# Expert stages: gathers and first weights earlier; ffn stages: two up chunks before the norm's root, first tap on ScalarE

## The chip, the cores and the metric

The kernel runs on one core of a Trainium2 chip. The metric is the device time of one execution in microseconds, taken as the median of several runs. TensorE multiplies matrices, VectorE, ScalarE and GpSimd work on SBUF (the first two on PSUM too), and SyncE (SP) issues nearly all transfers of weights.

## The reference

A small model in two blocks, one after the other, on 256 tokens of width 1024 (`x` is kept transposed, 8 tiles of 128 features). What is computed, cut to what matters:

```
first block:   x += g1 * MLA(modulate(norm(x)))             # with 256 context tokens
               x += g2 * MoE_0(modulate(norm(x)))           # 32 experts, top 2 in one of 4 groups
               x += g1 * short_conv(modulate(norm(x)))
               x += g2 * MoE_1(modulate(norm(x)))
               x = norm(x)
second block:  x += mamba2(norm(x));             x += ffn_0(norm(x))
               x += dilated_attention(norm(x));  x += ffn_1(norm(x))
               y = norm(x)

expert(t) = (silu(t @ w_gate) * (t @ w_up)) @ w_down
ffn(h)    = (silu(gate) * val) @ w_down,   gate, val = causal_conv3(h @ w_up)   # 2 x 2816 columns
norm(x)   = x * rsqrt(mean(x*x) + 1e-6) * gain
```

All data are float32. The tolerance asks for more than one pass of TensorE's rounded format, so the dense products use split values.

## The kernel before

**Engines and stages.** Each engine has one program, a list of stages: mla, expert stage 0, conv, expert stage 1, ssm, ffn 0, dilated, ffn 1. The order of the work on each engine is the order in which a stage's method writes it, and each engine executes its program in that order. Engines meet through counting semaphores; `at(name)` is the count at which a named step is done. `k.meet` at a stage's head waits for the end of the stage before on all four engines.

**Split products.** A weight chunk of 2 MiB is fetched into a ring of six 2 MiB slots by SP. ScalarE rounds it (`round_scalar`, L297, or in four pieces, `round_piece_scalar`, L312) into the next slot, VectorE subtracts (`rest_vector`, L303, in pieces L320), and a product is three passes: high weights by high values, high by low, low by high (`product3`, L584). `first_linear3_tensor` (L618, L619, L624) does the same for a stage's first chunk, k tile by k tile, as the values come. Values are split in the same way: ScalarE rounds (L680), VectorE subtracts (L668).

**Norms.** Squares of the residual tiles are made by ScalarE as the tiles come (in most stages GpSimd adds them, L487), TensorE adds over the features (L495, L497), ScalarE takes the root (L652), VectorE the reciprocal (L657), and then VectorE scales the eight tiles (L661, L699).

**Expert stage.** The router's logits and 80 small VectorE operations give places and shares. The rows of four experts (a team) are gathered by products with a 0/1 matrix (`gather`, L1307) and copied from PSUM by VectorE (`turned_x`, L1668). The four banks in which all experts' results are summed are opened by a product with zeros (`open_tensor`, L1344) between the ranks and the first gather. Then for every expert: gate and up (L1328), transposes, down (L1337), sum (L1352). Expert weights take half slots in order; SP waits for the half to be free (L347). Each stage has a further part behind a branch, for experts with more than 64 rows; the flag is zero here. The next stage's first chunk is fetched by that stage, behind the branch, and its pieces 0 and 1 are rounded by ScalarE around the root.

**Ffn.** Eleven up chunks of two output rows m each (128 gate and 128 value features per row), then six down chunks. TensorE leaves gate and value of a row in one PSUM bank. ScalarE copies it (L2744, L2749) to `PB`; VectorE makes three taps (L2783 the first, L2786 the other two, for gate and value); ScalarE takes silu (L2726); GpSimd multiplies (`h`, L2808); ScalarE rounds (L2728); GpSimd subtracts (L2810). In ScalarE's program row m's turn is: round a chunk (m even), silu and high part of row m-2, copy of row m. The down product begins by waiting for the bank of every row.

Of the kernel before, what the change touches and what calls it, by code (L numbers as in the profile page):

```python
# [16 lines left out]
P = 128  # L17
# [3 lines left out]
HALF = SLOT // 2  # L21

# [479 lines left out]
class Kernel:  # L502
# [102 lines left out]
    def first_linear3_tensor(self, e, w, chunk, outs, weights, values, n_k, tiles, pieces=False):  # L605
# [6 lines left out]
        for i in range(n_k):  # L612
# [51 lines left out]
    def norm_parts_vector(self, e, w, tag, value, gain, high, low, chunk=None):  # L664
# [5 lines left out]
        for k in range(KD):  # L670
            self.norm_value_vector(e, w, tag, k, value, gain)
            if chunk and k % 2 and k > 1:
                chunk.rest_piece_vector(e, w, k // 2)
# [13 lines left out]
    def modulated_parts_vector(self, e, w, tag, layer, T, high, low, chunk=None):  # L687
# [9 lines left out]
        for k in range(KD):  # L697
# [3 lines left out]
            if chunk and k % 2 and k > 1:  # L701
                chunk.rest_piece_vector(e, w, k // 2)
# [514 lines left out]
class Moe:  # L1217
    def __init__(self, k, layer, T, cap, before):
# [12 lines left out]
        self.slots, self.zero = ar.take(P), ar.take(P)  # L1231
        self.zeros_by = k.mats[:, 0:4, :].rearrange("p m n -> p (m n)")
# [31 lines left out]
    def sync(self, e, w):  # L1264
# [8 lines left out]
        self.k.ring.close_halves()  # L1273
        self.more_sync(e, w)
# [81 lines left out]
    def tensor(self, e, w):  # L1356
# [38 lines left out]
        w.wait_ge(*pool.at(key, "zero"))  # L1395
        for b in range(KD // 2):
            _, emptied = banks.next(dve, key, "acc", b)
            banks.hold(key, "acc", b)
            w.wait_ge(*emptied)
        self.open_tensor(e)  # L1400
# [50 lines left out]
        for part in range(KD // 2):  # L1451
            gather(0, part)
        for x in range(EXPERTS):
# [21 lines left out]
    def scalar(self, e, w):  # L1475
# [52 lines left out]
        self.then.first_chunk().round_piece_scalar(e, w, 0)  # L1528
        k.root_scalar(e, w, ("moe", layer), SEQ, eps=NORM_EPS * NORM_EPS if layer else NORM_EPS)
        self.then.first_chunk().round_piece_scalar(e, w, 1)  # L1530
        act.mark("end", key)

    def vector(self, e, w):
# [157 lines left out]
        for x in range(EXPERTS):  # L1691
# [7 lines left out]
            if x % TEAM == TEAM - 1 and x // TEAM + 2 < EXPERTS // TEAM:  # L1699
                places_of(x // TEAM + 2)  # L1700
        w.wait_ge(*pe.at(key, "sum", EXPERTS - 1))
# [5 lines left out]
        self.then.first_chunk().rest_piece_vector(e, w, 0)  # L1707
# [1671 lines left out]
```

## Time and profile before

| | |
|---|---|
| median of 3 runs | 2243.75 us (2243.53 to 2244.0) |
| profiled execution | 2242.49 us, its span 2240.7 us |
| TensorE busy | 2109.5 us, 94% of the span |
| VectorE, ScalarE, GpSimd busy | 1003.7, 718.4, 244.7 us |
| read from memory | 613.69 MB, 274 GB/s over the span |
| mean granted TensorE clock | 0.975 of full |

The profile is of one execution. Times in rows are microseconds from the span's start. "L584" is a line of the kernel. In a timeline a row is: start, duration, engine, line, operation, output<-inputs, shape, count, and in brackets how long the engine had been idle and what released it. A row with a count above 1 merges instructions that follow each other.

### The profile page before, as it was taken

To read this page: it belongs to the slowest core of one execution; us is meant where nothing else is said; L and a number is where in the kernel's file an instruction comes from. 1 tells how busy PE (TensorE), PEld (TensorE's weight loads), DVE (VectorE), ACT (ScalarE), POOL (GpSimd) and SP (SyncE) were. 2 spreads that over 40 slices of the span, in tenths; PEclk is the share of its full clock that TensorE was granted. 3 is DMA by queue.
4 is the path that set the end of the run, shared out by engine and by line. 5 is a ranking of instruction groups with operands and counts; after the bars stand their busy time and mean duration, and the time that the engine had idled before them with its cause. 6 is when DMAs were issued, how large, how long until landed. Compare 5 with 4: busy or idle time off the path is not lost. (4 is left out here: it accounts for less than half of the span.)

```text
span 2240.7 us, 31183 instructions
## 1 busy us (share of the span) xinstructions
PE 2109.5 (94%) x13462; PEld 1481.8 (66%) x13462; DVE 1003.7 (45%) x1653; ACT 718.4 (32%) x1079; POOL 244.7 (11%) x220
## 2 busy tenths in 40 slices
PE   5999999999999898999999988997899989998998
PEld 3845744444443696444444437975899989998997
DVE  3434411111111564111111107865479846777983
ACT  3234211111111442111111118855545534444552
POOL 0000000000000000000000000046125400002540
PEclk9999899999999999999999999999999999999999
DMA  9777599999999557999999985432345454434542
GB/s 326 252 273 275 227 410 421 421 421 421 421 421 421 192 204 304 417 421 421 422 420 421 421 352 191 151 113 76 113 151 189 174 196 122 113 113 151 188 171 94
DMA packets 216208, 616.86 MB, mean 275 GB/s; under 512 B 20224, under 2 KB 107392, under 8 KB 166656
## 3 DMA queue, kind: packets, MB, share of 16 engines
q1 hardware_dynamic: 208960, 612.01, 71.0%
q10 hardware_dynamic: 7104, 2.76, 0.5%
q8 instruction: 110, 1.80, 0.3%
q14 instruction: 34, 0.28, 0.0%
HBM read 613.69 MB, written 1.05 MB: 274 GB/s over the span
## 5 line engine op out<-in xcount | busy, mean ns | idle before, releaser
L1328 PE MATMUL bank<-ring,arena 128*64 128x512 f32 x2048 | 454.4, 593 | 12.4 <-DMA ring<-in_moe_w_up 12.3
L584 PE MATMUL bank<-normed_rounded,ring_rounded 128*128 128x256 f32 x3424 | 415.5, 283 | 5.0 <-ACT normed_rounded L680 3.4
L584 PEld LDWEIGHTS bank<-normed_rounded,ring_rounded 128*128 128x128 f32 x3424 | 411.2, 189 | 6.9 <-issue 4.3
L1328 PEld LDWEIGHTS bank<-ring,arena 128*64 128x64 f32 x2048 | 149.4, 137 | 305.8 <-issue 304.9
L1674 DVE TENSOR_TENSOR arena<-arena,bank 64x512 f32<-64x512 f32 x64 | 43.6, 681 | 659.3 <-ACT arena L1498 659.3
L303 DVE TENSOR_TENSOR ring_rounded<-ring,ring_rounded 128x4096 fp32r<-128x4096 f32 (+2 forms) x66 | 286.6, 4345 | 115.2 <-ACT ring_rounded L297 115.0
L584 PE MATMUL bank<-arena_rounded,ring_rounded 128*128 128x256 f32 x2336 | 290.9, 284 | 6.8 <-ACT arena_rounded L1927 2.6
L584 PEld LDWEIGHTS bank<-arena_rounded,ring_rounded 128*128 128x128 f32 x2336 | 283.3, 190 | 9.2 <-ACT arena_rounded L1927 3.4
L297 ACT ACTIVATE ring_rounded<-ring 128x4096 fp32r<-128x4096 f32 (+2 forms) x66 | 227.7, 3450 | 39.4 <-DMA ring<-in_ffn_w_down 32.8
L1337 PE MATMUL bank<-ring,arena 128*64 128x512 f32 x1024 | 233.8, 598 | 3.8 <-ACT arena L1505 3.8
L1498 ACT ACTIVATE arena<-bank 64x512 f32<-64x512 f32 x64 | 38.1, 596 | 451.0 <-PE bank L1328 451.0
L1337 PEld LDWEIGHTS bank<-ring,arena 128*64 128x64 f32 x1024 | 67.8, 136 | 122.4 <-issue 109.6
L572 PEld LDWEIGHTS bank<-mats,arena 128*128 128x128 f32 (+2 forms) x662 | 85.0, 167 | 78.8 <-issue 66.5
L1352 PE MATMUL bank<-arena 64*128 64x256 f32 x1024 | 127.8, 388 | 1.4 <-ACT arena L1512 1.4
L1512 ACT ACTIVATE arena<-bank 128x512 f32<-128x512 f32 x64 | 38.3, 599 | 275.2 <-PE bank L1337 275.2
L572 PE MATMUL bank<-mats,arena 128*128 128x128 f32 (+2 forms) x662 | 102.9, 278 | 8.5 <-POOL arena L2414 5.4
L1352 PEld LDWEIGHTS bank<-arena 64*128 64x128 f32 x1024 | 93.2, 186 | 23.7 <-issue 11.6
L2786 DVE SCALAR_TENSOR_TENSOR arena<-arena,cols 128x256 f32<-128x256 f32 x176 | 94.4, 537 | 6.3
L2810 POOL TENSOR_TENSOR arena_rounded<-arena,arena_rounded 128x256 fp32r<-128x256 f32 x44 | 93.5, 2125 | 23.3 <-ACT arena_rounded L2728 23.3
L1307 PE MATMUL bank<-arena_rounded 128*128 128x256 f32 x512 | 78.4, 298 | 0.0
L1307 PEld LDWEIGHTS bank<-arena_rounded 128*128 128x128 f32 x512 | 65.7, 190 | 5.0 <-issue 1.2
L1505 ACT ACTIVATE arena<-bank 128x256 f32<-128x256 f32 x64 | 24.7, 386 | 132.5 <-PE bank L572 132.5
(274 smaller groups left out, 2101.4 us busy)
## 6 DMA issues: line engine op xcount, KB each, us to landing
ring<-in_moe_w_gate SPq DMA_DIRECT2D x128, 1024.0 KB, 16.6
ring<-in_moe_w_up SPq DMA_DIRECT2D x128, 1024.0 KB, 18.7
ring<-in_moe_w_down SPq DMA_DIRECT2D x128, 1024.0 KB, 18.4
ring<-in_w_mod SPq DMA_DIRECT2D x24, 2048.0 KB, 11.8
ring<-in_ffn_w_up SPq DMA_DIRECT2D x44, 1024.0 KB, 6.9
ring<-in_ssm_w_in SPq DMA_DIRECT2D x12, 2048.0 KB, 8.3
ring<-in_ffn_w_down SPq DMA_DIRECT2D x10, 2048.0 KB, 8.0
ring<-in_conv_w_in SPq DMA_DIRECT2D x6, 2048.0 KB, 9.1
```

Of the source, the lines that this page charges most:

```text
L297: e.activation(ring.rounded[(self.number + 1) % RING][:, 0:n].bitcast(F32R), ring.slots[self.number % RING][:, 0:n], ACT.Copy).then_inc(*s ...
L303: e.tensor_tensor(ring.rounded[slot][:, 0:n].bitcast(F32R), ring.slots[slot][:, 0:n], ring.rounded[(self.number + 1) % RING][:, 0:n], ALU. ...
L572: return e.transpose(out, in_, self.mats[0:rows, 0, 0:rows])
L584: end = e.matmul(out, lhs.bitcast(F32R), rhs.bitcast(F32R), start=start and n == 0 and k == 0, stop=stop and n == 2 and k == n_k - 1)
L1307: end = e.matmul(out, f[:, t, feats].bitcast(F32R), mine[:, t, hot].bitcast(F32R), start=t == 0 and f is self.f_high, stop=t == self.NT - ...
L1328: ends[i] = e.matmul(bank[rows, :], xt[:, n * KD // 2 + j, :], weights[:, j, :], start=n == 0 and j == 0, stop=n == 1 and j == KD // 2 - 1)
L1337: end = e.matmul(bank[n * cap:(n + 1) * cap, :], self.ht[x][:, k, :], weights[:, i, n * 512:(n + 1) * 512], start=k == 0, stop=k == KF - 1)
L1352: end = e.matmul(self.acc(kk), self.y[x][rows, i * P:(i + 1) * P], self.back[x][rows, :], start=False, stop=last and kk % 2 == 1)
L1512: e.activation(self.y[x % 2], banks.of(key, "y", x)[:, :], ACT.Copy).then_inc(*act.up(key, "y", x))
L1674: e.tensor_tensor(h, h, banks.of(key, "h", x)[0:cap, :], ALU.mult).then_inc(*dve.up(key, "h", x))
L2786: e.scalar_tensor_tensor(buf, self.PB[:, s, j, q:q + T], w3[:, q:q + 1], buf, ALU.mult, ALU.add).then_inc(*dve.up())
L2810: e.tensor_tensor(self.H_low[:, m, :].bitcast(F32R), self.H[:, m, :], self.H_high[:, m, :], ALU.subtract).then_inc(*pool.up(key, "h low", m))
```

## The change

- Expert stages: the zero product that opens the sum banks uses a rounded zero tile, in one pass, and stands behind the first team's four gathers. VectorE copies the four gathered parts first, and then does weights, shares and tables. The ring is advanced to a whole turn, and the next stage's first chunk is fetched ahead of the branch; ScalarE rounds its pieces 0 and 1 behind the last expert's result, and VectorE subtracts piece 0 before and piece 1 after the residual update. The loops of the branch's part are merged into one.
- Ffn stages: the stage before (`prior`) also makes `raw` = residual times gain, without the root, split in high and low. Up chunks 0 and 1 are products with `raw`; chunk 0 starts without `meet`, and closes the stage before (`close_tensor`) after its second k tile. Chunk 1 is rounded in the stage before, in pieces. Rows 0 to 3 leave PSUM on VectorE, multiplied by the reciprocal root (`normed`). Chunks 2 and on use the normed values as before; chunk 2 is rounded in turn 0 and no chunk in turn 2.
- Ffn stages: the first tap of each row, for gate and value, is a scaled copy on ScalarE.

```diff
@@ first_linear3_tensor, after the products of k tile i
+            if between and i < n_k - 1:
+                between(i)
@@ Moe.sync, Moe.open_tensor
         self.k.ring.close_halves()
+        while self.k.ring.number % RING:
+            self.k.ring.skip()
+        self.then.first_chunk().fetch(e, w)
         self.more_sync(e, w)
...
+        zero = self.zero_rounded.bitcast(F32R)
         for b in range(KD // 2):
-            e.matmul(self.k.banks.of(self.key, "acc", b)[:, :], self.zero, self.zeros_by, start=True, stop=False)
+            e.matmul(self.k.banks.of(self.key, "acc", b)[:, :], zero, across(zero, BANK // P), start=True, stop=False)
@@ Moe.tensor
-        w.wait_ge(*pool.at(key, "zero"))
-        ...
-        self.open_tensor(e)
...
         for part in range(KD // 2):
             gather(0, part)
+        w.wait_ge(*pool.at(key, "zero"))
+        ...
+        self.open_tensor(e)
@@ Moe.scalar
             result(x)
+        for q in (0, 1):
+            self.then.first_chunk().round_piece_scalar(e, w, q)
...
         self.more_scalar(e)
-        self.then.first_chunk().round_piece_scalar(e, w, 0)
         k.root_scalar(e, w, ("moe", layer), SEQ, eps=NORM_EPS * NORM_EPS if layer else NORM_EPS)
-        self.then.first_chunk().round_piece_scalar(e, w, 1)
@@ Moe.vector
-        for part, between in enumerate((weights, shared, tables, lambda: self.last_steps.close_vector(e, w))):
+        for part in range(KD // 2):
             turned_x(0, part)
-            between()
+        weights()
+        shared()
+        tables()
+        self.last_steps.close_vector(e, w)
@@ Ffn, new; called by ssm and dilated behind plain_vector and square_scalar of tile m
+    def raw_vector(self, e, w, m):
+        w.wait_ge(*k.dve.now())
+        e.tensor_scalar(self.raw[:, m, :], k.X[:, m, 0:SEQ], k.col("ffn_norm")[:, self.layer, m:m + 1], None, ALU.mult
+                        ).then_inc(*k.dve.up(self.key, "raw value", m))
+    def raw_scalar(self, e, w, m):
+        w.wait_ge(*k.dve.at(self.key, "raw value", m))
+        e.activation(self.raw_parts[0](m).bitcast(F32R), self.raw[:, m, :], ACT.Copy).then_inc(*k.act.up(self.key, "raw high", m))
+    def raw_low_vector(self, e, w, m):
+        w.wait_ge(*k.act.at(self.key, "raw high", m))
+        e.tensor_tensor(self.raw_parts[1](m).bitcast(F32R), self.raw[:, m, :], self.raw_parts[0](m), ALU.subtract
+                        ).then_inc(*k.dve.up(self.key, "raw low", m))
@@ Ffn.tensor
-        k.meet(w, self.before)
...
-        k.first_linear3_tensor(e, w, first, outs, (high, low), self.x_parts, KD, k.norm_tiles(key))
+        k.first_linear3_tensor(e, w, first, outs, (high, low), self.raw_parts, KD, self.raw_ready,
+                               between=lambda i: self.prior.close_tensor(e, w) if i == 1 else None)
         for n, chunk in enumerate(self.w_up[1:], 1):
+            values, tiles = (self.raw_parts, None) if n == 1 else (self.x_parts, k.norm_tiles(key) if n == 2 else None)
@@ Ffn.scalar, turn m
-            if m % 2 == 0:
+            if m == 0:
+                self.w_up[2].round_scalar(e, w)
+            elif m % 2 == 0 and m > 2:
                 (self.w_up + self.w_down)[m // 2 + 1].round_scalar(e, w)
...
+            w.wait_ge(*(act if m >= 4 else dve).at(key, "up", m))
+            for j in range(2):
+                e.activation(self.acc[:, s, j, :], self.PB[:, s, j, 0:T], ACT.Copy,
+                             scale=taps[:, self.layer, j * KFF + m, 0:1]).then_inc(*act.up(key, "tap", m, j))
@@ Ffn.vector, turn m
+            w.wait_ge(*act.at(key, "tap", m))
             for j in range(2):
                 buf, w3 = self.acc[:, s, j, :], taps[:, self.layer, j * KFF + m, :]
-                e.tensor_scalar(buf, self.PB[:, s, j, 0:T], w3[:, 0:1], None, ALU.mult).then_inc(*dve.up())
...
+            if m < 2:
+                normed(m + 2)
@@ Ssm.vector, last part (Dilated.vector alike, with the low parts of tiles 0 to 3 and 4 to 7 together)
+            for m in (2 * n - 2, 2 * n - 1):
+                if m >= 0:
+                    self.then.raw_low_vector(e, w, m)
             for m in (2 * n, 2 * n + 1):
                 k.plain_vector(e, w, "ssm out", m)
-        k.root_vector(e, w, "ssm out", T)
+                self.then.raw_vector(e, w, m)
+        self.then.raw_low_vector(e, w, 6)
+        self.then.raw_low_vector(e, w, 7)
+        for q in range(4):
+            if q == 2:
+                k.root_vector(e, w, "ssm out", T)
+            self.then.w_up[1].rest_piece_vector(e, w, q)
```

## Rows read from the trace of the kernel before

**Rows 1.** The page, busy time of the engines.
```profile
PE 2109.5 (94%) x13462; PEld 1481.8 (66%) x13462; DVE 1003.7 (45%) x1653; ACT 718.4 (32%) x1079; POOL 244.7 (11%) x220
```
**Rows 2.** Timelines, TensorE at the start of both expert stages.
```profile
264.79 6.65 PE L1344 MATMUL bank<-mats,arena 128*128 128x512 f32 x8 [1.90 <-DVE arena_rounded L1578]
270.87 4.47 PE L1307 MATMUL bank<-arena_rounded 128*128 128x256 f32 x32
275.27 7.09 PE L1328 MATMUL bank<-ring,arena 128*64 128x512 f32 x32
...
870.33 5.96 PE L1344 MATMUL bank<-mats,arena 128*128 128x512 f32 x8 [1.90 <-DVE arena_rounded L1578]
...
880.13 7.09 PE L1328 MATMUL bank<-ring,arena 128*64 128x512 f32 x32
```
**Rows 3.** Stretches: length, busy of PE, PEld, DVE, ACT, POOL, clock, DMA share, GB/s.
```profile
260.60:270.80 10.20, 8.30 (x17) 4.67 (x18) 3.56 (x10) 0.00 (x0) 0.00 (x0) 0.50 0.98 410
```
**Rows 4.** Waits of TensorE: us in total, times, longest.
```profile
PE bank L1328 <- DMA ring<-in_moe_w_up: 12.3, 18, 1.3
```
**Rows 5.** Timelines, ScalarE at the end of both expert stages.
```profile
742.42 3.16 ACT L432 ACTIVATE arena<-residual 128x256 f32<-128x256 f32 x8 [1.10 <-DVE residual L1713]
...
746.37 1.28 ACT L312 ACT_TABLE_LOAD   x1 [0.79 <-issue]
747.66 1.06 ACT L312 ACTIVATE ring_rounded<-ring 128x1024 fp32r<-128x1024 f32 x1
...
750.03 0.38 ACT L652 ACTIVATE rstd<-bank 128x256 f32<-128x256 f32 x1
...
1354.22 1.06 ACT L312 ACTIVATE ring_rounded<-ring 128x1024 fp32r<-128x1024 f32 x1 [1.38 <-DMA ring<-in_ssm_w_in]
...
1356.59 0.38 ACT L652 ACTIVATE rstd<-bank 128x256 f32<-128x256 f32 x1
```
**Rows 6.** First ffn's start, second ffn's last row: timeline and one stretch.
```profile
1644.09 0.55 PE L618 MATMUL bank<-normed_rounded,ring_rounded 128*128 128x256 f32 x1 [3.40 <-ACT normed_rounded L680]
...
1644.10:1649.60 5.50, 5.50 (x26) 5.50 (x27) 4.77 (x14) 5.50 (x8) 0.82 (x1) 0.50 0.46 150
...
1658.28 0.39 ACT L2744 ACTIVATE arena<-bank 128x256 f32<-128x256 f32 x1 [0.56 <-PE bank L624]
...
2051.25 0.39 ACT L2744 ACTIVATE arena<-bank 128x256 f32<-128x256 f32 x1 [0.56 <-PE bank L624]
```
**Rows 7.** Up loop of ffn 0: ScalarE's timeline; stretch of L584 alone (PE, PEld).
```profile
1704.47 3.62 ACT L297 ACTIVATE ring_rounded<-ring 128x4096 fp32r<-128x4096 f32 x1
1707.99 0.40 ACT L2726 ACTIVATE arena<-arena 128x256 f32<-128x256 f32 x1
1709.48 0.42 ACT L2728 ACTIVATE arena_rounded<-arena 128x256 fp32r<-128x256 f32 x1 [1.09 <-POOL arena L2808]
1709.81 0.58 ACT L2749 ACTIVATE arena<-bank 128x512 f32<-128x512 f32 x1
1710.28 0.41 ACT L2726 ACTIVATE arena<-arena 128x256 f32<-128x256 f32 x1
1715.11 0.42 ACT L2728 ACTIVATE arena_rounded<-arena 128x256 fp32r<-128x256 f32 x1 [4.42 <-POOL arena L2808]
...
1715.91 3.62 ACT L297 ACTIVATE ring_rounded<-ring 128x4096 fp32r<-128x4096 f32 x1
...
1738.02:1749.41 11.39, 11.39 (x98) 11.39 (x97) 1.00 0.58 186
```
**Rows 8.** Up loop of ffn 0, timelines: VectorE's L303 and GpSimd's products.
```profile
1662.21 4.42 DVE L303 TENSOR_TENSOR ring_rounded<-ring,ring_rounded 128x4096 fp32r<-128x4096 f32 x1
1663.99 3.25 POOL L2808 TENSOR_TENSOR arena<-arena 128x256 f32<-128x256 f32 x1 [19.07 <-ACT arena L2726]
...
1708.46 0.98 POOL L2808 TENSOR_TENSOR arena<-arena 128x256 f32<-128x256 f32 x1 [3.44 <-ACT arena L2726]
...
1708.76 4.97 DVE L303 TENSOR_TENSOR ring_rounded<-ring,ring_rounded 128x4096 fp32r<-128x4096 f32 x1
```
**Rows 9.** Ssm's input rows, ScalarE's timeline: copy, first tap, silu of another row.
```profile
1397.68 0.37 ACT L2321 ACTIVATE arena<-bank 128x256 f32<-128x256 f32 x1
1398.08 0.51 ACT L2324 ACTIVATE arena<-arena,cols 128x256 f32<-128x256 f32 x1
1398.49 0.49 ACT L2287 ACTIVATE arena<-arena,cols 128x256 f32<-128x256 f32 x1
```
**Rows 10.** Timeline, TensorE at the start of ffn 0's down product.
```profile
1772.94 13.25 PE L584 MATMUL bank<-arena_rounded,ring_rounded 128*128 128x256 f32 x110 [0.78 <-ACT arena L2749]
```

More of the change, by code:

```diff
@@ L21 @@
 HALF = SLOT // 2
+RAW = 8192
 D = 1024
@@ L603, in linear3_tensor, with first_linear3_tensor @@
         pe.mark("free", chunk.number)
-    def first_linear3_tensor(self, e, w, chunk, outs, weights, values, n_k, tiles, pieces=False):
+    def first_linear3_tensor(self, e, w, chunk, outs, weights, values, n_k, tiles, pieces=False, between=None):
         pe, (high, low) = self.pe, weights
@@ L1452, in tensor @@
             gather(0, part)
+        w.wait_ge(*pool.at(key, "zero"))
+        for b in range(KD // 2):
+            _, emptied = banks.next(dve, key, "acc", b)
+            banks.hold(key, "acc", b)
+            w.wait_ge(*emptied)
+        self.open_tensor(e)
         for x in range(EXPERTS):
@@ new lines, in more_tensor @@
+            with e.Fori(0, (self.n_blocks - 1) * EXPERTS, 1) as it:
+                e.wait_ge(*self.more_count("vector", it, 2))
+                awake()
+                for tile in range(KD):
+                    self.gather_tensor(e, x_turned[:, tile * self.cap:(tile + 1) * self.cap], tile, slice(0, self.cap),
+                                       self.mine[0])
+                self.back_tensor(e, turned, 0).then_inc(matmul, 1)
+                e.wait_ge(*self.more_count("vector", it, 4))
+                awake()
+                e.wait_ge(*self.more_count("landed", it, 48))
+                awake()
+                for half in range(2):
+                    tiles = slice(half * KD // 2, (half + 1) * KD // 2)
+                    end = self.gate_up_tensor(e, rows, self.rows_of(0), half, gate[:, tiles, :], up[:, tiles, :])[1]
+                end.then_inc(matmul, 1)
+                e.wait_ge(*self.more_count("vector", it, 5))
+                awake()
+                self.turn_h_tensor(e, turned, 0).then_inc(matmul, 1)
+                e.wait_ge(*self.more_count("scalar", it, 2))
+                awake()
+                self.down_tensor(e, x_turned, 0, range(KF), down).then_inc(matmul, 1)
+                e.wait_ge(*self.more_count("scalar", it, 3))
+                awake()
+                self.open_tensor(e)
+                self.sum_tensor(e, 0, True).then_inc(matmul, 1)
+                e.wait_ge(*self.more_count("vector", it, 6))
+                awake()
@@ L1892, in sync @@
     def sync(self, e, w):
-        for chunk in self.w_in + self.w_out:
+        for chunk in self.w_in[1:] + self.w_out:
             chunk.fetch(e, w)
@@ L2059, in sync @@
     def sync(self, e, w):
-        for chunk in self.w_xbc + self.w_z + self.w_out:
+        for chunk in self.w_xbc[1:] + self.w_z + self.w_out:
             chunk.fetch(e, w)
@@ L2397, in scalar @@
             self.squares.square_scalar(e, w, m, k.X[:, m, 0:T], dve.at("ssm out", m))
+            self.then.raw_scalar(e, w, m)
+            self.then.w_up[1].round_piece_scalar(e, w, m - 6)
         k.root_scalar(e, w, "ssm out", T)
+        for q in (2, 3):
+            self.then.w_up[1].round_piece_scalar(e, w, q)
         act.mark("end", "ssm")
@@ L3193, in vector @@
             k.plain_vector(e, w, "att y", m)
+            self.then.raw_vector(e, w, m)
+        for m in range(4):
+            self.then.raw_low_vector(e, w, m)
         self.then.prepare_vector(e, w)
@@ L3196, in vector @@
             k.plain_vector(e, w, "att y", m)
-        k.root_vector(e, w, "dilated out", T)
+            self.then.raw_vector(e, w, m)
+        for m in range(4, KD):
+            self.then.raw_low_vector(e, w, m)
+        for q in range(4):
+            if q == 2:
+                k.root_vector(e, w, "dilated out", T)
+            self.then.w_up[1].rest_piece_vector(e, w, q)
         dve.mark("end", "dilated")
```

121 lines of the change are left out of this document (60 added, 61 removed).

## The prediction

> **What bounds the kernel now.** I read the page first, then windows and timelines around each place that the diff touches. TensorE is busy for 94% of the span [rows 1], so time can only come from the few stretches in which it stands still, works without need or runs at its lower clock, and time is lost wherever another engine's loop becomes longer than TensorE's. Three kinds of place matter.
>
> *Start of an expert stage.* TensorE opens the four sum banks with eight f32 passes (L1344), then gathers the first team, then starts the first expert: 264.79, 270.87 and 275.27 us in the first stage, 870.33 and 880.13 in the second [rows 2]. The opening falls into a stretch in which half the clock is granted (0.50, the 1.2 GHz level) behind idle moments of TensorE, and the DMA engines, busy at 0.98 there, fill the ring [rows 3]. From the first expert on both TensorE and the queues work without a pause, and near the end TensorE begins to wait for weights, 12.3 us in 18 waits over both stages [rows 4]. Both chains hang on the first expert's start: its first half frees the ring's first slot.
>
> *Change of stage.* Behind the experts the root waits in ScalarE's queue: table load, a piece of the next chunk, another table load, root at 750.03; in the second stage the piece waits another 1.38 us for its data and the root is at 1356.59 [rows 5]. At the ffn's start TensorE waits 3.40 us and then works for 5.5 us at half clock; its first chunk's last result is fetched at 1658.28, in the second ffn at 2051.25 [rows 6].
>
> *The ffn's up loop.* One chunk (two output rows m) takes TensorE 11.39 us, without idle time. ScalarE's round of the same work goes from 1704.47 to 1715.91, 11.44 us, and is full: rounding, silu, wait for GpSimd's product, high part, copy [rows 7]. VectorE is full as well. So there are three loops of one length, and what is added to any of them shows.
>
> **The change, part by part.**
>
> 1. *Gathers ahead of the opening, opening in fp32r.* The 32 gathers can start when the low parts are there, 0.5 us behind the point where L1344 starts now. With the clock's rise about where it is (5 us into the busy stretch, between the two stages' cases), some 24 gathers go at 0.21 us (26 matmuls in 5.5 us, [rows 6]) and 8 at 0.14 (4.47 us for 32, [rows 2]), 6.2 us; the opening is then four single passes of 512 columns at full clock, twice the 256 columns of 0.116 us (98 in 11.39 us, [rows 7]), 0.9 us. The first expert starts 0.5 + 6.2 + 0.9 = 7.6 us after the old start of L1344 against 10.5 and 9.8 now: about -2.6 us, twice, -5. If the clock stays down for all of it the sum is 0.5 + 6.8 + 1.8 = 9.1, a gain of 1 each; if it never falls it is 4.6 each. VectorE's small routing work, now behind the four copies, is 4.7 us and hidden by the first expert's 7.09 us of matmuls [rows 2]. GpSimd's rounding of the zero tile is hidden by the routing. Since both chains start at the first expert, the gain reaches the stage's end.
>
> 2. *First chunk fetched ahead of the branch, two pieces rounded before the squares.* SP issues it into slot 0 behind the last weights, it lands before the last expert's end, where the queues now stand empty. On ScalarE the pieces are 2 x 1.06 us before the squares, which wait 1.10 us for VectorE today: squares 1.0 us later. Behind the branch one table load (1.28) and one piece (1.06) go: root 2.34 - 1.0 = 1.3 us earlier; in the second stage 1.38 more, 2.7. Sum -4 [rows 5]. The Trainium skill (ScalarE: Activation LUTs, Table sets: the hidden batching unit) says that copy is in every table set, by which the load at 746.37, ahead of a copy, would not be the copy's; if it vanished with it, 1.28 us more would be gained in each stage. I do not count that. The queues' order changes nothing else on SP: the later chunks of the next stage are issued earlier too, with nobody waiting for them.
>
> 3. *Up chunks without the root.* TensorE goes on with chunk 0 and closes the squares after its second k tile. Gone are the 3.40 us of waiting, about 2.5 us of half clock (5.5 us at half speed) and some of the closing's own waits. Against it: each pair of output rows in the stage before puts two more products and two subtractions on VectorE and two copies on ScalarE, 0.35 to 0.42 us each, in a chain VectorE - ScalarE - rounding - VectorE that the ssm's output loop repeats. I add up 3 us until w_up[0]'s low part is there, so TensorE waits 0.7 us, then 1.5 us for the last square. Chunk 0 ends at 1653.5 instead of 1658.3: -4.8. Behind the attention only the second half of the rows is in that chain: 2044.3 instead of 2051.2, -6.9. Chunk 1 needs its low part 8 us later than VectorE has it. Sum -11.7.
>
> 4. *Up rows leave by VectorE (first four), first tap on ScalarE.* VectorE sheds its L2783 and has room again. ScalarE gets two scaled copies per row. The nearest rows are the ssm's: a tap starts 0.40 behind its own PSUM copy and the next one 0.41 later [rows 9]; with the ffn's longer copy (0.58 plus wait) copy and taps take 0.61 + 0.82 = 1.43 us where the copy took 0.47: +1.92 us per chunk. Worse is what VectorE's room does. Today VectorE comes to its rounding difference L303 at 1708.76, 0.67 us after the rounding copy's end (1704.47 + 3.62), just behind GpSimd's start on the product for which ScalarE waits, and that wait is 1.09 us [rows 7, 8]. With four L2783 less per chunk VectorE is through its taps before the copy ends; L303 then starts with the copy's end, 0.35 us ahead of the product. The case is in the trace, at the loop's start, when VectorE was not yet behind: L303 at 1662.21 for 4.42 us, the product at 1663.99 took 3.25 us and ended 0.6 us after it [rows 8]. ScalarE's chunk then is: rounding 3.53, silu and product 5.15 (until 3.65 + 4.42 + 0.61 from the chunk's start), high 0.33, copy and taps 1.43, silu and an unblocked product 1.4 (0.47, and 0.8 to 1.0), high 0.33, copy and taps 1.43: 13.6 us, against TensorE's 11.39. The same addition over today's rows gives their 11.44.
>
> TensorE asks for the low part of a chunk two thirds into its first row. By my dates w_up[3]'s comes just in time; w_up[4] to w_up[10], seven chunks, come 2.2 us later each: 15.4 us per ffn. Then the down product cannot start before ScalarE has copied row 21, which now stands behind a blocked product, two taps and a rounding piece: about 6.0 us of idle TensorE instead of 0.78 [rows 10], +5.2, and an idle time longer than the 3.40 us before the half-clock stretch of [rows 6] should bring half clock again, +2 (0 to 3.4). Later down chunks have slack. Sum 22.6 per ffn, +45.
>
> **Sum:** -5 - 4 - 11.7 + 45.2 = +24.5 us. The profiled execution took 2242.49 us (span 2240.70 and 1.8 around it), the median is 2243.75; I add to the median: **2268 us**.
>
> **Rivals.**
> - *R1, everything hidden (the other side).* If ScalarE's chunk stays under 11.39 us, no part of item 4 shows and 20.7 us are gained: 2223 us. It needs GpSimd's product to begin before L303; then the wait is 1 us instead of 4.7, ScalarE's chunk 10.0. For it: today the order is that way round in nearly every chunk. Against it: that order hangs on the 0.67 us that VectorE is late, and item 4 takes over 1.5 us per chunk from VectorE. The Trainium skill (SBUF — State Buffer, Who interferes with whom) says that the engine which issues first holds the shared port for its whole instruction; the trace agrees, with 3.25 us against 0.98, and so by that rule too the order decides. Items 3 and 4 cancel at a chunk of 12.2 to 12.3 us or so; below that the kernel is faster.
> - *R2, the loop is longer, but less.* A chunk of 12.5 to 12.9 us (a product let in now and then, shorter taps), and TensorE's slack at the loop's start larger: +5 to +10, 2251.
> - *R3, the expert stages give nothing.* The clock rises later because the gathers are the first steady work, and the queues, not TensorE, carry the stage: +9 on the forecast, 2277. For it: TensorE's 12.3 us of waiting for weights. Against it: their chain starts at the same event.
> - *R4, worse:* half clock in every 2.2 us stall, or a late w_up[3]: 2288.
>
> **Chances:** forecast 0.60 (own range 2256 to 2280), R1 0.17, R2 0.12, R3 0.06, R4 0.05. A measurement of this kernel can tell about 0.2%, 4.5 us, from no change. Range 2247 to 2284, which leaves out R1 and half of R4. Faster 0.19 (R1 and a little of R2), same 0.04, slower 0.77.
>
> **What would show it.** Item 1: L1328 of the first expert 2 to 3 us closer to L1390 in both stages. Item 2: no L312 between the branch and the root, one table load there. Item 3: no idle TensorE before the first L618 of an ffn, clock 1.0 there. Item 4: in the up loop L303 and ScalarE's L297 every 13.6 us, GpSimd's L2808 at over 4 us once per chunk, seven waits of TensorE for L303 of about 2.2 us in each ffn, and one of about 6 us for the last copy. The forecast is wrong if L2808 stays near 1 us or L297 stays at 11.4 us.

## The result and the profile after

The changed kernel takes **2265.66 us** (median, 2260.51 to 2268.83), the kernel before 2243.64 in the same rounds: ratio 1.0099, 95% interval 1.0078 to 1.0119, 22 us slower. The forecast was 2268, range 2247 to 2284. The profiled execution took 2265.92 us (span 2263.9). TensorE's busy time is as before; what grew is what it waits for:

```profile
PE 2108.9 (93%) x13454; PEld 1484.6 (66%) x13454; DVE 981.2 (43%) x1615; ACT 754.6 (33%) x1175; POOL 242.3 (11%) x222
```

The waits of TensorE over the span (us in total, times, longest) name the places; against them the kernel before had 0.4 us in one wait for the difference of a rounded chunk, L303, which is L304 now:

```profile
PE bank L585 <- DVE ring_rounded L304: 25.6, 16, 1.8
PE bank L1333 <- DMA ring<-in_moe_w_up: 11.6, 17, 1.7
PE bank L585 <- ACT arena L2797: 11.1, 2, 5.5
PE bank L619 <- ACT normed_rounded L714: 4.2, 1, 4.2
```

Read as milestones of TensorE (starts in both timelines, us), the two profiled executions differ by:

| | before | after | difference |
|---|---|---|---|
| first expert, stage 0 | 275.27 | 271.90 | -3.4 |
| conv's first product | 753.88 | 748.16 | -5.7 |
| first expert, stage 1 | 880.13 | 876.04 | -4.1 |
| ssm's first product | 1360.35 | 1353.62 | -6.7 |
| ffn 0: chunk 0 done | 1658.08 | 1645.91 | -12.2 |
| ffn 0: down product | 1772.94 | 1780.43 | +7.5 |
| attention's first product | 1844.65 | 1854.43 | +9.8 |
| ffn 1: chunk 0 done | 2051.05 | 2052.97 | +1.9 |
| ffn 1: down product | 2165.90 | 2187.24 | +21.3 |
| last product | 2229.64 | 2252.96 | +23.3 |

**Expert stages.** TensorE's timeline at both starts (answers to [rows 2]): gathers, opening in four passes (L1350), first expert (L1333).

```profile
264.46 6.58 PE L1312 MATMUL bank<-arena_rounded 128*128 128x256 f32 x32 [2.40 <-DVE arena_rounded L1584]
270.88 1.09 PE L1350 MATMUL bank<-arena_rounded 128*128 128x512 f32 x4
271.90 7.09 PE L1333 MATMUL bank<-ring,arena 128*64 128x512 f32 x32
...
868.59 6.59 PE L1312 MATMUL bank<-arena_rounded 128*128 128x256 f32 x32 [2.41 <-DVE arena_rounded L1584]
875.01 1.10 PE L1350 MATMUL bank<-arena_rounded 128*128 128x512 f32 x4
876.04 7.09 PE L1333 MATMUL bank<-ring,arena 128*64 128x512 f32 x32
```

From the first gather to the first expert it is 7.44 and 7.45 us; the forecast was 7.1. ScalarE at both ends (answers to [rows 5]): one table load (L655) in place of two, and the second stage's root (L655) now waits for the squares' sum.

```profile
736.33 1.99 ACT L313 ACTIVATE ring_rounded<-ring 128x1024 fp32r<-128x1024 f32 x2
...
743.01 1.28 ACT L655 ACT_TABLE_LOAD   x1 [0.73 <-issue]
744.31 0.38 ACT L655 ACTIVATE rstd<-bank 128x256 f32<-128x256 f32 x1
...
1347.17 1.28 ACT L655 ACT_TABLE_LOAD   x1
1349.86 0.38 ACT L655 ACTIVATE rstd<-bank 128x256 f32<-128x256 f32 x1 [1.41 <-PE bank L451]
```

**Up loop of ffn 0.** One chunk in ScalarE's timeline, from rounding to rounding (answer to [rows 7]):

```profile
1676.25 3.61 ACT L298 ACTIVATE ring_rounded<-ring 128x4096 fp32r<-128x4096 f32 x1
1679.76 0.40 ACT L2778 ACTIVATE arena<-arena 128x256 f32<-128x256 f32 x1
1684.94 0.42 ACT L2780 ACTIVATE arena_rounded<-arena 128x256 fp32r<-128x256 f32 x1 [4.78 <-POOL arena L2881]
1685.27 0.58 ACT L2797 ACTIVATE arena<-bank 128x512 f32<-128x512 f32 x1
1685.88 0.91 ACT L2801 ACTIVATE arena<-arena,cols 128x256 f32<-128x256 f32 x2
1686.70 0.40 ACT L2778 ACTIVATE arena<-arena 128x256 f32<-128x256 f32 x1
1687.95 0.42 ACT L2780 ACTIVATE arena_rounded<-arena 128x256 fp32r<-128x256 f32 x1 [0.85 <-POOL arena L2881]
1688.28 0.58 ACT L2797 ACTIVATE arena<-bank 128x512 f32<-128x512 f32 x1
1688.89 0.91 ACT L2801 ACTIVATE arena<-arena,cols 128x256 f32<-128x256 f32 x2
1689.70 3.61 ACT L298 ACTIVATE ring_rounded<-ring 128x4096 fp32r<-128x4096 f32 x1
```

VectorE's difference and GpSimd's two products of that chunk, from their timelines (answers to [rows 8]):

```profile
1679.89 4.43 DVE L304 TENSOR_TENSOR ring_rounded<-ring,ring_rounded 128x4096 fp32r<-128x4096 f32 x1 [1.47 <-ACT ring_rounded L298]
...
1680.24 4.67 POOL L2881 TENSOR_TENSOR arena<-arena 128x256 f32<-128x256 f32 x1 [4.37 <-ACT arena L2778]
...
1687.18 0.74 POOL L2881 TENSOR_TENSOR arena<-arena 128x256 f32<-128x256 f32 x1 [1.01 <-ACT arena L2778]
```

The chunk is 13.45 us. The difference starts as soon as the rounding copy ends, 0.35 us ahead of the product, and the product takes 4.67 us instead of 0.74. TensorE's timeline shows what that leaves of its 11.39 us loop, and the down product's start (answer to [rows 10]):

```profile
1657.27 13.45 PE L585 MATMUL bank<-normed_rounded,ring_rounded 128*128 128x256 f32 x112
1670.92 11.65 PE L585 MATMUL bank<-normed_rounded,ring_rounded 128*128 128x256 f32 x96 [0.20 <-DVE ring_rounded L304]
1684.37 11.65 PE L585 MATMUL bank<-normed_rounded,ring_rounded 128*128 128x256 f32 x96 [1.80 <-DVE ring_rounded L304]
...
1780.43 9.77 PE L585 MATMUL bank<-arena_rounded,ring_rounded 128*128 128x256 f32 x61 [5.54 <-ACT arena L2797]
```

### The profile page after: what moved, and what is told of

It reads as the page before. It is cut to its first block and busy times, and to the rows that moved or that the text cites. A ratio compares the mean times of both kernels' runs of the same rounds, so it can differ in the third digit from the quotient of the medians.

```text
span 2263.9 us, 31234 instructions
## 1 busy us (share of the span) xinstructions
PE 2108.9 (93%) x13454; PEld 1484.6 (66%) x13454; DVE 981.2 (43%) x1615; ACT 754.6 (33%) x1175; POOL 242.3 (11%) x222
## 5 line engine op out<-in xcount | busy, mean ns | idle before, releaser
L1333 PE MATMUL bank<-ring,arena 128*64 128x512 f32 x2048 | 454.2, 593 | 11.8 <-DMA ring<-in_moe_w_up 11.6
L585 PE MATMUL bank<-normed_rounded,ring_rounded 128*128 128x256 f32 x3232 | 397.1, 284 | 30.0 <-DVE ring_rounded L304 25.2
L585 PEld LDWEIGHTS bank<-normed_rounded,ring_rounded 128*128 128x128 f32 x3232 | 389.6, 189 | 35.2 <-DVE ring_rounded L304 28.4
L1333 PEld LDWEIGHTS bank<-ring,arena 128*64 128x64 f32 x2048 | 149.2, 137 | 305.4 <-issue 304.0
L585 PE MATMUL bank<-arena_rounded,ring_rounded 128*128 128x256 f32 x2528 | 318.0, 286 | 16.4 <-ACT arena L2797 11.1
L304 DVE TENSOR_TENSOR ring_rounded<-ring,ring_rounded 128x4096 fp32r<-128x4096 f32 (+1 forms) x64 | 269.2, 4206 | 135.9 <-ACT ring_rounded L298 135.9
L585 PEld LDWEIGHTS bank<-arena_rounded,ring_rounded 128*128 128x128 f32 x2528 | 310.5, 193 | 18.8 <-ACT arena L2797 11.4
L298 ACT ACTIVATE ring_rounded<-ring 128x4096 fp32r<-128x4096 f32 (+1 forms) x64 | 220.4, 3444 | 44.5 <-DMA ring<-in_ffn_w_down 36.6
L2857 DVE SCALAR_TENSOR_TENSOR arena<-arena,cols 128x256 f32<-128x256 f32 x176 | 102.0, 580 | 54.5 <-ACT arena L2801 48.9
L2881 POOL TENSOR_TENSOR arena<-arena 128x256 f32<-128x256 f32 x44 | 99.5, 2260 | 133.7 <-ACT arena L2778 133.7
L1312 PEld LDWEIGHTS bank<-arena_rounded 128*128 128x128 f32 x512 | 70.4, 204 | 8.8 <-DVE arena_rounded L1584 5.1
```

Source lines behind the costliest of these rows:

```text
L298: e.activation(ring.rounded[(self.number + 1) % RING][:, 0:n].bitcast(F32R), ring.slots[self.number % RING][:, 0:n], ACT.Copy).then_inc(*s ...
L304: e.tensor_tensor(ring.rounded[slot][:, 0:n].bitcast(F32R), ring.slots[slot][:, 0:n], ring.rounded[(self.number + 1) % RING][:, 0:n], ALU. ...
L585: end = e.matmul(out, lhs.bitcast(F32R), rhs.bitcast(F32R), start=start and n == 0 and k == 0, stop=stop and n == 2 and k == n_k - 1)
L1312: end = e.matmul(out, f[:, t, feats].bitcast(F32R), mine[:, t, hot].bitcast(F32R), start=t == 0 and f is self.f_high, stop=t == self.NT - ...
L1333: ends[i] = e.matmul(bank[rows, :], xt[:, n * KD // 2 + j, :], weights[:, j, :], start=n == 0 and j == 0, stop=n == 1 and j == KD // 2 - 1)
L2857: e.scalar_tensor_tensor(buf, self.PB[:, s, j, q:q + T], w3[:, q:q + 1], buf, ALU.mult, ALU.add).then_inc(*dve.up())
```

## The experiments

Twelve runs of eleven kernels (experts_again is experts_only once more). "At like clock" is worked out: over all 162 timed executions, compared within each kernel, 0.001 of mean granted clock goes with 1.34 us, and each mean is moved by that to a clock of 0.976. There the kernel before (63 executions) is at 2241.9 and the changed one at 2264.2. This measure has a flaw: where a change itself lets the clock stay up or fall, it takes that part of the effect away.

"Behind the ssm" is a second measure, from the profiled execution alone: from the end of the ssm's last product of weights to the start of the very last product, the stretch that holds both ffn stages and the attention. The kernel before takes 590.6 us for it, the changed kernel 621.2. Four other executions with the same code there agree with 590.6 within 0.3 us; a fifth, open_f32, took 593.6. What lies ahead of the stretch differs more: the ssm's last product ends at 1625.2 to 1634.1 us in the eight profiled executions that have both of the expert stages' parts, with the opening in the rounded format.

| kernel | median us | ratio to before, 95% | at like clock | behind the ssm |
|---|---|---|---|---|
| tap_vector | 2232.67 | 0.9959 (0.9945 to 0.9973) | 2232.7 | 590.3 |
| tap_only | 2278.88 | 1.0168 (1.0151 to 1.0185) | 2275.1 | 631.2 |
| late_rest | 2257.48 | 1.0072 (1.0055 to 1.0089) | 2257.0 | 612.8 |
| gated_rest | 2244.37 | 1.0006 (0.9996 to 1.0016) | 2245.4 | 601.9 |
| experts_only | 2231.38 | 0.9947 (0.9934 to 0.9960) | 2232.8 | 590.4 |
| gather_only | 2242.77 | 0.9997 (0.9988 to 1.0005) | 2238.3 | 590.4 |
| fetch_only | 2239.88 | 0.9984 (0.9975 to 0.9993) | 2239.3 | 590.3 |
| raw_only | 2240.97 | 0.9988 (0.9976 to 0.9999) | 2240.9 | 588.3 |
| tap_four | 2229.67 | 0.9939 (0.9924 to 0.9955) | 2232.9 | 587.9 |
| pieces_rest | 2230.07 | 0.9945 (0.9932 to 0.9957) | 2231.4 | 584.9 |
| experts_again | 2231.92 | 0.9949 (0.9936 to 0.9962) | 2232.2 | 590.3 |
| open_f32 | 2240.05 | 0.9986 (0.9975 to 0.9996) | 2239.2 | 593.6 |

**tap_vector: the change without its fourth part.**

```diff
@@ Ffn.scalar, Ffn.vector, turn m, against the changed kernel
-                e.activation(self.acc[:, s, j, :], self.PB[:, s, j, 0:T], ACT.Copy, scale=taps[...])   # ScalarE
+                e.tensor_scalar(buf, self.PB[:, s, j, 0:T], w3[:, 0:1], None, ALU.mult)                # VectorE
```

The lines are shortened; VectorE's own wait for the product of row m-4, which the kernel before has, comes back with the tap.

> The changed kernel with the first tap of all rows back on VectorE; everything else of the change stays. Theory (the order of VectorE's rounding difference and GpSimd's product makes the up loop long): ScalarE's chunk falls from 13.46 us back to about 11.4 us, no wait of TensorE for the difference, the wait before the down product back to about 0.8 us; 2266 - 2 x (7 x 2.07 + 4.8 + 2.3) = about 2223 us. Rival (the four rows that leave PSUM by VectorE and the two chunks from the raw values carry a good part of the loss): 2235 to 2255 us.

2232.67 us: 33 us under the changed kernel, 10 us over the 2223 that the theory gave and 2 under the rival's range. The 13.45 us loop and the 5.5 us wait are gone. What was not foreseen is one wait, before the fourth chunk (w_up[3]) of each ffn. TensorE's timeline:

```profile
1675.85 24.37 PE L585 MATMUL bank<-normed_rounded,ring_rounded 128*128 128x256 f32 x180 [2.87 <-DVE ring_rounded L304]
```

The stretch behind that wait (length, busy of PE, PEld, DVE, ACT, POOL, clock, DMA share, GB/s):

```profile
1675.85:1679.20 3.35, 3.35 (x15) 3.35 (x16) 3.21 (x7) 2.78 (x3) 1.27 (x2) 0.50 0.90 284
```

TensorE waits 2.87 us and then works at half clock (the 1.2 GHz level), until 1682.0; in the second ffn the wait is 2.62 us. In the changed kernel it was 0.20 us. From the end of chunk 0 to the down product ffn 0 takes 120.7 us here and 114.9 in the kernel before, so the 5 us gained at chunk 0 are gone there.

**tap_only: the fourth part on the kernel before.** The same edit the other way round, nothing else.

> The kernel before with nothing changed but the first tap, for all rows on ScalarE. Theory: the loop is 13.5 us per chunk here too, stalls of about 2.1 us in 7 to 9 chunks of each ffn and about 5.5 us before each down product: 2244 + 2 x (7 to 9 x 2.07 + 4.8 + 2.3) = 2287 to 2296 us. Rival (the loss comes from the tap together with the raw chunks): within 10 us of 2244.

+37 us, 8 to 17 under what was expected. The mechanism is there unchanged (GpSimd's timeline, with its product at L2811):

```profile
1699.54 4.68 POOL L2811 TENSOR_TENSOR arena<-arena 128x256 f32<-128x256 f32 x1 [4.38 <-ACT arena L2726]
```

But TensorE enters the loop later and so waits less for the same loop of ScalarE. Its waits from 1600 to 1800 us:

```profile
PE bank L584 <- DVE ring_rounded L303: 9.7, 7, 1.8
PE bank L584 <- ACT arena L2750: 4.0, 1, 4.0
```

What counts behind a loop that ScalarE carries is when ScalarE enters it. It begins to round w_up[3] 34.1 us after the ssm's last product here and 31.0 us after it in the changed kernel, and the down product starts 151.8 and 148.6 us after it: of the 5 us that the raw chunks gain at chunk 0, about 3 are kept.

**late_rest: VectorE makes the difference behind the taps.**

```diff
@@ Ffn.vector, turn m, against the changed kernel
-            elif m % 2 == 0 and m > 2:
-                (self.w_up + self.w_down)[m // 2 + 1].rest_vector(e, w)
...
             dve.mark(key, "taps", m)
+            if m % 2 == 0 and m > 2:
+                (self.w_up + self.w_down)[m // 2 + 1].rest_vector(e, w)
```

> The changed kernel with one line moved: in the up loop VectorE makes the rounding difference of the chunk behind the two taps of row m, not before them. No engine gets more or less work. Theory (order): the difference starts some 4.9 us after the rounding copy's end, when the product of the turn is long done; the product takes 0.74 us in both turns of a chunk, ScalarE's chunk would be 9.5 us by itself and is held at TensorE's 11.39 us; the low part comes about 4.9 us later, TensorE has 0 to 2 us left for it. About 2223 us, up to 2240 us if the low part comes late. Rival (work): the two scaled copies per row add 1.92 us to a full ScalarE, 11.44 + 1.92 = 13.36 us per chunk, whatever VectorE's order: 2266 us.

2257.48: between the two, and above the 2240 allowed. Order against work is decided in the trace: all 44 products are short, and ScalarE waits for TensorE now, not for GpSimd. But a new loop has closed: TensorE's row, ScalarE's copy, taps, difference, TensorE's next chunk, 12.84 us long. The product's own rows (durations: min, median, max in ns):

```profile
L2881 POOL TENSOR_TENSOR arena<-arena x44: 735/745/975, 1653.1 to 2185.4; 128x256 f32<-128x256 f32 x44
```

TensorE's timeline:

```profile
1686.54 11.66 PE L585 MATMUL bank<-normed_rounded,ring_rounded 128*128 128x256 f32 x96 [1.18 <-DVE ring_rounded L304]
1699.39 11.66 PE L585 MATMUL bank<-normed_rounded,ring_rounded 128*128 128x256 f32 x96 [1.19 <-DVE ring_rounded L304]
```

The "0 to 2 us" that TensorE was to have left for the low part were -1.2 in seven chunks of each ffn. The longest wait of the same kind is the first, before w_up[3], with 5.74 us in ffn 0 and 6.18 in ffn 1. So this run shows that the product is short again in the other order; its time also holds the cost of a low part that comes late.

**gated_rest: one wait more.**

```diff
             elif m % 2 == 0 and m > 2:
+                w.wait_ge(*pool.at(key, "h", m - 2))
                 (self.w_up + self.w_down)[m // 2 + 1].rest_vector(e, w)
```

> The changed kernel with one wait more: in the up loop VectorE starts the difference of a chunk only when GpSimd's product of the row two before is done. Theory (order): the first product of a chunk takes 0.74 us in place of 4.67; but then the difference (4.42 us) blocks GpSimd's low part and the product of the second turn behind it: chunk of about 12.0 us, TensorE's stalls about 0.6 us each in place of 2.07, the wait before the down product about 3 to 5 us: 2266 - 2 x 7 x 1.45 - 0 to 4 = 2242 to 2246 us. Rival (work): 2266 us or more, for the wait only makes the difference later.

2244.37, in the range of the order theory, 22 us under its rival: a wait added to VectorE makes the kernel 21 us faster. GpSimd's timeline shows the block moved on to the low part (L2884) behind the product (L2882), as expected; the chunk is 12.46 us (12.0 expected). TensorE's waits for the low part are about 0.8 us each (0.6 expected), the one before the first down product 2.31 (3 to 5).

```profile
1697.56 0.75 POOL L2882 TENSOR_TENSOR arena<-arena 128x256 f32<-128x256 f32 x1 [4.38 <-ACT arena L2778]
1698.84 4.52 POOL L2884 TENSOR_TENSOR arena_rounded<-arena,arena_rounded 128x256 fp32r<-128x256 f32 x1 [0.53 <-ACT arena_rounded L2780]
1703.32 0.92 POOL L2882 TENSOR_TENSOR arena<-arena 128x256 f32<-128x256 f32 x1
```

**pieces_rest: the difference in four instructions, no wait added.**

```diff
             elif m % 2 == 0 and m > 2:
-                (self.w_up + self.w_down)[m // 2 + 1].rest_vector(e, w)
+                ...                     # shortened; one wait for the rounding copy, as in rest_vector
+                for q in range(4):      # a quarter of the chunk's columns each
+                    e.tensor_tensor(low[:, cols], slots[:, cols], high[:, cols], ALU.subtract)
```

> The changed kernel with the difference of each chunk of the up loop made in four instructions of a quarter each, back to back, no wait added and all taps on ScalarE. Theory (GpSimd is shut out by a running instruction of VectorE, not by VectorE's queue): it gets in at the first border of two pieces, its product takes 1.3 to 1.9 us in place of 4.67, ScalarE's chunk would be some 10.5 us and TensorE's 11.39 us holds: 2221 to 2226 us. Rival (it stays shut out while VectorE issues back to back): product 4.7 us or more, chunk 13.5 us or more, 2264 us.

2230.07: 36 us under the changed kernel by cutting one instruction in four, with every tap still on ScalarE. VectorE's and GpSimd's timelines:

```profile
1701.02 6.28 DVE L2853 TENSOR_TENSOR ring_rounded<-ring,ring_rounded 128x1024 fp32r<-128x1024 f32 x4 [0.52 <-ACT ring_rounded L298]
...
1701.37 1.49 POOL L2889 TENSOR_TENSOR arena<-arena 128x256 f32<-128x256 f32 x1 [4.86 <-ACT arena L2778]
1703.38 1.15 POOL L2891 TENSOR_TENSOR arena_rounded<-arena,arena_rounded 128x256 fp32r<-128x256 f32 x1 [0.53 <-ACT arena_rounded L2780]
1705.12 1.10 POOL L2889 TENSOR_TENSOR arena<-arena 128x256 f32<-128x256 f32 x1 [0.59 <-ACT arena L2778]
```

GpSimd gets in between the pieces: product 1.49 us, and all four GpSimd instructions of a chunk run in 6.5 us. VectorE pays for it, 6.28 us in place of 4.43, which it has since it makes four taps fewer. ScalarE's chunk is TensorE's 11.39 us. The theory missed by 4 to 9 us: there is one wait before w_up[3] in each ffn, as in tap_vector, of 2.05 and 2.35 us, and TensorE works near half clock right behind it (0.52 over the 3.6 us from 1673.2).

**tap_four: first tap on ScalarE for rows 0 to 3 alone.** In the changed kernel the tap goes back to VectorE for m >= 4.

> The changed kernel with the first tap on ScalarE for rows 0 to 3 alone, and on VectorE from row 4 on. Theory: what the raw chunks gain at the ffn's start (5.0 and 6.1 us) was lost in the kernels with all taps on VectorE to one wait of 2.9 us for the low part of the fourth chunk and 3.4 us of half clock behind it; with the four taps on ScalarE, which is idle there, that wait is 0.2 us as in the changed kernel, and the loop behind it is TensorE's 11.39 us: some 11 us under the kernel with the expert stages' parts alone, 2242 - 9 - 11 = 2222 us. Rival (the loss sits elsewhere, or the loop starts in the order in which the product waits for the difference and stays there): 2231 to 2240 us.

2229.67, 8 us over the expectation and 1 us under the rival's range, so nearer to the rival. The wait before w_up[3] is 0.22 us as it should be, but 1.10 us of the same kind come one chunk later and the wait before the down product is 1.96 us (0.78 before). TensorE's timeline:

```profile
1669.90 11.66 PE L585 MATMUL bank<-normed_rounded,ring_rounded 128*128 128x256 f32 x96 [0.22 <-DVE ring_rounded L304]
1682.66 78.90 PE L585 MATMUL bank<-normed_rounded,ring_rounded 128*128 128x256 f32 x656 [1.10 <-DVE ring_rounded L304]
1763.52 55.72 PE L585 MATMUL bank<-arena_rounded,ring_rounded 128*128 128x256 f32 x456 [1.96 <-ACT arena L2797]
```

**raw_only: the third part alone.** The kernel before with the raw chunks, taps on VectorE.

> The kernel before with the third part alone: two up chunks from the residual times gain, the root closed inside the first, rows 0 to 3 scaled on their way out of PSUM by VectorE; all taps on VectorE. Theory: chunk 0 ends 5.0 us earlier in the first ffn and 6.1 us in the second, and the loop behind it is TensorE's 11.39 us: 2244 - 11 = 2233 us, and with the 7 us of the expert stages it makes the 2223 us expected of the changed kernel with its taps on VectorE. Rival (the added work in the ssm's and attention's last phases, or VectorE's later entry into the loop, gives some back): 2236 to 2244 us.

-2.6 us by the medians, -1.0 at like clock, -2.3 behind the ssm, where -11 was expected: the theory is wrong on the worth of this part, the rival right. It has the same wait before w_up[3], 2.85 us in ffn 0 and 3.17 in ffn 1.

**gather_only, fetch_only, experts_only, experts_again: the expert stages' parts.**

> The kernel before with the first part alone: gathers ahead of the opening, opening in one pass of the rounded format, VectorE's copies first. Theory: the first expert starts 3.4 us earlier in the first stage and 1 to 3 us earlier in the second (the changed kernel's trace: 3.37 and, behind a shift of the stages, 4.09 in all): 2244 - 5 = 2239 us. Rival (queues, not TensorE, carry the stage): 2244 us.

> The kernel before with the second part alone: first chunk of the next stage fetched ahead of the branch, two pieces rounded behind the last expert. Theory: last expert's result to first product of the next stage 2.4 us shorter in the first stage and 1.7 us in the second: 2244 - 4 = 2240 us. Rival (the stretch is carried by the branch and the root's own chain): 2243 to 2244 us.

> The kernel before with the expert stages' two parts alone (gathers ahead of the opening in the rounded format; first chunk fetched ahead of the branch, two pieces rounded before the squares). Theory from the changed kernel's trace: the ssm's end lies 7.2 us earlier than before, and nothing behind it takes that back: 2244 - 7.2 = 2236.5 us. Rival (the stages behind take it back by their clock or waits): 2244 us.

> The kernel with the expert stages' parts alone once more, beside the others of this call. If both parts' gains in place (2.5 us before the first expert of each stage, 2.35 and 1.7 to 3.1 us between a stage's last expert and the next product) are all there is, 2242 - 9.5 = 2232.5 us; if the sum of the two single runs at like clock is right, 2236 us.

fetch_only (2239.88) and experts_again (2231.92) came out as their theories said, experts_only (2231.38) 5 us under its own. gather_only (2242.77) did not: it lies nearer to its rival than to the 2239 expected, though its first experts start as early after the ranks as in the other kernels.

By the medians the two parts give 0.8 and 3.6 us alone and 12 together, which no sum explains. The clock goes with a part of that: gather_only ran at a mean clock of 0.9728 over its 11 executions, the kernel before at 0.9753. Why it ran lower is not shown. At like clock they give 3.6, 2.7 and together 9.1 to 9.7. In place, in all the traces with both parts, the stretch from a stage's last ranks to its first expert is 1.5 to 3.5 us shorter, from the last expert's down product to the next stage's first 2.35 us shorter in stage 0 and 1.7 to 3.1 in stage 1. The remaining 3 us between the sum of the two and both together stay open.

**open_f32: the gathers first, the opening still in f32.** experts_only with the old eight-pass product behind the gathers.

> The kernel with the expert stages' parts alone, but the opening behind the gathers stays in f32, eight passes of 512 columns. Theory (the gain of the first part lies in the format, the order alone is worth nothing, since both forms keep TensorE busy): the first expert starts 2.2 us (full clock) to 3.3 us (partly half clock) later in each stage, 2232.5 + 5 = 2237 to 2239 us. Rival (the order gives it: the clock rises earlier, or VectorE's copies run beside the opening): within 1 us of the kernel with the format.

2240.05 against 2231.92, 1 us over the theory's range and far from the rival: the format carries most of the first part. TensorE's timeline of both stages:

```profile
270.43 3.60 PE L1347 MATMUL bank<-mats,arena 128*128 128x512 f32 x8
...
874.18 3.60 PE L1347 MATMUL bank<-mats,arena 128*128 128x512 f32 x8
```

3.60 us at full clock against 1.09, so 2.5 us per stage; from the ranks to the first expert it is 12.35 and 12.39 us, against 13.4 and 12.4 before. The other 2 to 3 us of its loss fit the 3.3 us that its profiled execution takes more behind the ssm, where its code is that of the kernel before; why it does is not shown.

## Why the prediction came out right, and where it did not

**What bounds, items 1 and 2** (forecast -9): -7.2 us at the end of the ssm in the profiled execution (its last product ends at 1639.0 before, 1631.8 after), -9.1 to -9.7 at like clock in the two runs of these parts alone. R3 is out. Details were off: the 32 gathers took 6.4 us for 6.2, since the clock rose at their end and not before the last eight. Behind the last expert's down product, stage 0's next product comes 2.36 us earlier where 1.3 was forecast, since the two pieces did not delay the end of the squares; stage 1's comes 1.65 earlier where 2.7 was forecast, because the root waits for the squares' sum on TensorE. One table load is gone with its piece, as counted.

**Item 4, the mechanism**: as argued from one product of the kernel before. L304 starts 0.35 us ahead of the product, L2881 takes 4.67 us once per chunk, ScalarE's chunk is 13.45 us (forecast 13.6), the wait before the down product 5.54 us (6.0). The simple sum of added work, 11.44 + 1.92 = 13.36 us, would have given nearly the same chunk from another cause. late_rest, gated_rest and pieces_rest separate them: the same work in another order, with another wait, or in four instructions takes 2257, 2244 and 2230 us. The rule cited from the Trainium skill (SBUF — State Buffer, Who interferes with whom), that the engine which issues first holds the shared port for its whole instruction, is what these runs show, 4.67 us against 0.74; pieces_rest shows that the "whole instruction" is one instruction, not VectorE's run of them.

**The sum per ffn**, from the milestones. First ffn: chunk 0 done 5.0 us earlier (forecast 4.8); from there to the down product +19.7 (15.4 + 5.2 = 20.6); down product to the next stage +2.3 (2). Second ffn: -6.2 (6.9), +19.4 (20.6), +2.0 (2). The expert stages and ssm -7.2, the attention -1.7 (not foreseen, and within what the clock moves). Together +23.3 us for a forecast of +24.5. The clock did as forecast at both places: 1.00 through chunk 0 in both ffn stages, and 0.50 and 0.54 over the first 5 us of the two down products, behind the long wait.

**What was wrong** is the reading of item 3 as a gain of its own. "Sum -11.7" holds only up to the end of chunk 0. Against experts_again, tap_four has chunk 0 done 14.1 us after the ssm's last product, not 18.9; but from there to the down product it takes 118.6 us for 114.9, and the down stage 73.2 for 71.7. Nothing of the 5 us is left in ffn 0, about 3 us over the attention and ffn 1. Three loops of one length mean that TensorE cannot run ahead. ScalarE begins to round w_up[3] 31.0 us after the ssm's last product in the changed kernel, in tap_four and in experts_again alike. In the kernel before the low part of w_up[3] is there about 3.4 us before TensorE asks for it (the difference ends at 1679.4; TensorE asks at about 1682.8, which is worked out as two chunks of 11.39 us and a third of a row behind 1658.08). In tap_vector TensorE asks 4.8 us earlier and the low part comes 1.4 us later, which gives the wait of 2.87 us; the half clock behind the wait takes some 3 us more. The prediction said that what is added to any of the loops shows; it should have said too that of what is taken from one, only the slack of the others is gained.

In the sum this did little harm, since item 4's dates were worked out from the early entry: part of the 5 us came back as stalls there. From the end of chunk 0 to the down product the slow loop costs 17.8 us in tap_only and 19.7 in the changed kernel. Taken singly the terms are -1.0 (raw_only), +33.2 (tap_only) and, in the change, about +31.7 for both over the expert stages' parts alone, at like clock; behind the ssm they are -2.3, +40.6 and +30.9. The two measures differ by 7 us on tap_only, so how much of the raw chunks' 11.7 us the changed kernel keeps, 1.5 or 10, stays open.

**Also wrong:** TensorE asks for the low part of a chunk not "two thirds into its first row" but about one third in (after the high passes of the row's first half): in late_rest it goes on at 1686.54 and the row's copy can start at 1690.65, 4.1 us of the row's 5.7 later. R1's time of 2223 us was reached by no version; 2230 was.

**Clearly better than both kernels**, by 9 us or more, are four versions between 2229.67 and 2232.67 us. tap_four and pieces_rest have the lowest medians, but at like clock they, tap_vector and the expert stages' parts alone lie within 1.5 us of each other: by the run times the simple version without raw chunks and without moved taps has nearly all of the gain. Behind the ssm tap_four is 2.5 and pieces_rest 5.4 us shorter than experts_again, in one execution each. Whether that is a gain in every execution stays open, since the part ahead of it varies more than that.

## What to carry to other kernels

Where VectorE and GpSimd both work on SBUF in one loop, look at which of them starts first in each turn before giving one of them less to do: 1.5 us of relief per chunk on VectorE put a 4.4 us instruction ahead of a 0.7 us one and cost 16 us per ffn. A long instruction on VectorE beside a short one on GpSimd on which others wait is best cut in pieces. And a loop that three engines fill equally gives little back for an earlier start of one of them (2.3 us of 11 in raw_only); look for the second engine's entry time and its slack before crediting the first one's.

## What the runs showed of the hardware

- GpSimd's product (256 columns) beside VectorE's difference (4096 columns, 4.43 us): 4.67 us when it starts 0.35 us behind it, 0.74 with no difference running, 1.49 when the difference is cut in four; the four pieces then take 6.28 us in all, 1.9 more than the one. In the other order, the kernel before, the product takes 0.98 us and the difference 4.97.
- The mean granted clock differs from run to run of one kernel (before: 0.972 to 0.979 over 63 runs) and time goes with it, 1.34 us per 0.001, which is most of the 2237 to 2250 us over which that kernel spreads. It also differs between kernels, 0.9728 in gather_only and 0.9774 in gated_rest; a part of that can be the kernel's own doing, as in raw_only, whose half clock at chunk 0 is gone. Differences of 2 or 3 us between kernels need the clock beside the time, and a stretch of the trace beside both.
- Eight f32 passes of 512 columns took 3.60 us and four in the rounded format 1.09 us, both at full clock, for the same four banks.
